# A seven-product group in the first two down-projection blocks, and shares that join the stream by adding transfers

## The chip, the cores and the metric

The kernel runs on one core of one Trainium2 chip. The metric is the device time of one execution in microseconds. Five engines work beside each other, each through its own program in order, and wait for each other by semaphores: PE (TensorE, matmuls), DVE (VectorE), ACT (ScalarE), POOL (GpSimd) and SP (SyncE, which here only issues transfers). Matmuls read SBUF and write PSUM, whose eight banks the kernel uses as `acc[0]`, `acc[1]` (two banks each) and `side` (four).

## The reference

The reference is a two-layer decoder trunk over 256 tokens with 2048 features: layer 0 is differential attention, layer 1 is attention over a shared latent K/V, and each layer ends in a squared-ReLU MLP with 8192 hidden features. The change is in the MLP only:

```
def sq_relu_mlp(h, w_up, w_down):
    return jnp.square(jax.nn.relu(h @ w_up)) @ w_down

x = x + sq_relu_mlp(rms_norm(x, mlp_norm_g[l]), w_up[l], w_down[l])
```

All is float32. The gains of the norm are in `opA` already, and the norm's per-token factor `rs` is applied where a product is added to the stream `xs`.

## The kernel before

**Halves.** The kernel gets float32 accuracy from three fast matmuls: each operand is split into a high part and a low part, and a product is high x high + high x low + low x high. A weight block is 2048 rows by 512 columns. SP loads it in four quads (`raw[:, r]`, 4 chunks of 128 rows, 1 MB each); each quad is two halves of two chunks. For each half ACT writes the high part (`whi`, L1080) and DVE subtracts it to make the low part (`wlo`, L1672); both are called `split(b, hf)`. `whi` and `wlo` are a ring of four halves, so ACT may write half n once PE has done half n - 4 (`pe_halves`). PE then does 12 matmuls of 128x512 for a half: 2 chunks, 2 token tiles, 3 products (`half_tok`, L595 to L597).

**Groups of seven products.** Where two weight blocks j and j+1 and the two token tiles form a 2x2 by 2x2 product, `seven` computes it with seven products instead of eight (Strassen's scheme in Winograd's form): 7 x 2 chunks x 3 = 42 matmuls (L828 to L830) instead of 48. Its names are B22, T1, B21, B11, T2, T3, T4, in PE's order. DVE makes the four weight sums in `w_sum` and in place in `raw` (L2199, L2202, L2209, L2213). Four of the seven weight operands go through the ring (ACT L1405, DVE L2188), three (T1, B11, T3) through `extra_hi` and `extra_lo` (ACT L1401, DVE L2182), which hold two; T3's high part takes T1's place and waits until PE has used it (`pe_extra`). The activations are combined too: `form_sums`, `form_high` and `form_low` make four sums and split them (`forms[0]`, `forms[1]`). Four of the products (T1, B11, T2, T3) land in the four `side` banks; they are shares of more than one output tile. ACT copies them out (`down_shared` in `junk` and `o_sb`, or `up_shared`), and `combine` on DVE turns them into the four tile sums by four 128x512 operations (L2105). The products that belong to one tile alone accumulate in `acc`.

**The MLP.** It runs in four quarters of the hidden features. In each quarter PE does four up blocks and four down blocks. Up blocks 2 and 3 of the first quarter and all up blocks of the others are done as `up_pair(q, i)`, with one seven-product group each. The results pass ReLU and square on ACT, are turned by DVE and by transfers (`up_turn`, `move_quads`, `hid_high`, `hid_low`) into `opB`. The down blocks are two stages. `first_down(q)` does down blocks 0 and 1, 16 plain halves in the order `DOWN_ORDER`. `pair(q)` does down blocks 2 and 3, with two seven-product groups in three of the quarters: four halves of block 2, group 0, two halves, group 1, two halves. After a block `add_scaled` (L2136) multiplies `acc` by `rs` and adds it to `xs`. The shares of `pair` are combined at its end, and `down_add` (L2251, two DVE operations over 128x1024) adds them to the stream in the next up pair. The last quarter has no group in its down blocks.

**Order.** All orders are written out by hand, per engine. PE runs the first three quarters in a `Fori` loop; ACT, DVE and SP are unrolled.

Of the kernel before, what the change touches and what calls it, by code (L numbers as in the profile page):

```python
# [39 lines left out]
NB = 512  # L40
# [45 lines left out]
IN_EXTRA = ("T1", "B11", "T3")  # L86
IN_RING = ("B22", "B21", "T2", "T4")
DOWN_ORDER = ((0, 0), (0, 1), (0, 2), (1, 0), (0, 3), (1, 1), (1, 2), (1, 3))
SUMS = {"T1": 1, "T3": 2, "T2": 3, "T4": 4}
PAIRS_UP = 2 * QUARTERS - 1  # L90
GROUPS = PAIRS_UP + 2 * (QUARTERS - 1)
SHARES = PAIRS_UP + QUARTERS - 1
# [3 lines left out]
def up_pairs(l, q, i):  # L96

    return PAIRS_UP * l + 2 * q - 1 + i


def up_groups(l, q, i):

    return GROUPS * l + 4 * q - 1 + i


def down_groups(l, q, g):
    return GROUPS * l + 4 * q + 1 + g


def up_shares(l, q, i):  # L110

    return SHARES * l + 3 * q - 1 + i


def down_shares(l, q):
    return SHARES * l + 3 * q + 1


def extra_place(l, at, form):

    return 2 * ((GROUPS * l + at + IN_EXTRA.index(form)) % 2)

# [37 lines left out]
def trunk(nc, x, positions, a_w_qkv, a_lambda, a_w_o, w_dkv, w_ukv, b_w_dq, b_w_uq, b_w_o, w_up, w_down,  # L160
# [11 lines left out]
    with ExitStack() as ctx:  # L172
# [196 lines left out]
        shared_sums = sem("shared_sums")  # L369
        shared_added = sem("shared_added")  # L370
# [17 lines left out]
        def _(sp):  # L388
# [53 lines left out]
            def mlp(l):  # L442
# [6 lines left out]
                def move_quads(q, j):  # L449

                    n = JB * (QUARTERS * l + q) + j
                    sp.wait_ge(sqT_done, n + 1)
                    if not (isinstance(n, int) and n == 0):
                        sp.wait_ge(hid_lo, 2 * n)
                    for a in range(4):
                        sp.dma_start(quads_moved[:, :, a, :], quads[32 * a:32 * a + 32, :]).then_inc(sq_moves, 16)

                def first_down(q):

                    b = B_MLP[l] + 2 * JB * q + JB  # L460
                    for k, (j, r) in enumerate(DOWN_ORDER):
# [5 lines left out]
                def pair(q):  # L467
# [3 lines left out]
                    for i, (j, r) in enumerate(order):  # L471
                        src = W_DOWN[l][:, KC * q + 4 * r:KC * q + 4 * r + 4, NB * j:NB * j + NB]
                        quad(b + i // 4, i % 4, src, later=int(i == 6))
# [61 lines left out]
        def _(pool):  # L535
# [21 lines left out]

            stream_scale(0)
            with pool.Fori(0, DA_PAIRS) as p:
                sub_norm(p)  # L560
            stream_scale(2)
            for k in range(2):
                pool.wait_ge(lat_ms, k + 1)
                nc.gpsimd.tensor_tensor(lrs[:, k, :], lms[:, k, :], neg_half[:, 0:TT], ALU.pow).then_inc(lat_rs, 1)
            for t in range(TT):
# [5 lines left out]
        def _(pe):  # L571
# [228 lines left out]
            def mlp(l, v_in):  # L800
# [3 lines left out]
                def seven(group, at, b, hf0, buf, c0, made, uses, opens, closes):  # L804
# [8 lines left out]
                    for f in FORMS:  # L813
                        shares = f in ("T1", "B11", "T2", "T3")
                        if f in IN_EXTRA:
                            pe.wait_ge(extra_lo_ready, len(IN_EXTRA) * group + IN_EXTRA.index(f) + 1)
                            hi, lo, place = extra_hi, extra_lo, extra_place(l, at, f)
# [4 lines left out]
                        first, last = opens and (shares or f == "B22"), closes and f != "B22"  # L822
                        if opens and f == "B22":
                            wait_bank(0, uses, 0)
# [8 lines left out]
                def shares_free(share):  # L833

                    if not (isinstance(share, int) and share == 0):
                        pe.wait_ge(shared_copied, 4 * share)

                def pair(q, uses):
# [4 lines left out]
                    shares_free(down_shares(l, q))  # L843
                    pe.wait_ge(form_lo, FORM_SETS * l + 2 * q + 3)
                    seven(down_groups(l, q, 0), 1, b, 4, opB, 8, [forms[0][:, i] for i in range(2)], uses[0], True, False)
                    for hf in range(2):
                        half_tok(b + 1, hf, 0, chunks_of(opB, 2 * hf), first=hf == 0, uses=uses[0], starts=(False, True))
                    seven(down_groups(l, q, 1), 2, b + 1, 2, opB, 12, [forms[1][:, i] for i in range(2)], None, False, True)
# [3 lines left out]
                def up_pair(q, i):  # L852
# [5 lines left out]
                    shares_free(up_shares(l, q, i))  # L858
                    pe.wait_ge(form_lo, FORM_SETS * l + 1)
                    seven(up_groups(l, q, i), i - 1, b, 6, opA, 0, x_forms, uses[0], True, True)  # L860
# [7 lines left out]
                def first_down(q):  # L868

                    b = B_MLP[l] + 2 * JB * q + JB  # L870
                    for k, (j, r) in enumerate(DOWN_ORDER):
# [1676 lines left out]
```

## Time and profile before

| | us |
|---|---|
| median of 3 runs | 1988.44 (1988.22 to 1989.09) |
| the profiled execution, its own time | 1988.36 |
| its span, from the first to the last instruction | 1986.6 |
| PE busy, 9128 matmuls | 1977.4 |
| DVE busy | 1582.4 |
| ACT busy | 1161.1 |
| POOL busy | 13.2 |

The busy times are sums over one execution; the engines work at the same time. PE's matmuls overlap each other, so the distance between their starts, not the duration of one, says how fast PE goes. A DVE or ACT operation likewise starts slightly before the one ahead of it has fully ended.

### The profile page before, as it was taken

How to read it: one execution, taken by the hardware profiler on the slowest of the kernel's cores; microseconds unless marked ns; L12 is line 12 of the kernel's file. 1: busy time of each engine (PE TensorE's matmuls, PEld its weight loads, DVE VectorE, ACT ScalarE, POOL GpSimd, SP SyncE). 2: the span in 40 equal slices, each digit the busy share in tenths (PEclk: the TensorE clock that was granted, in tenths of full speed). 3: DMA queues.
4: the chain of work that ended last, by engine and by line, in shares of the span. 5: the costliest groups of instructions: out<-in, count | busy, mean ns of one | idle time of the engine just before them, and what ended most of it. 6: DMA issues, size and time to landing. Idle time of an engine off the chain costs nothing.

```text
span 1986.6 us, 24882 instructions
## 1 busy us (share of the span) xinstructions
PE 1977.4 (100%) x9128; PEld 1651.8 (83%) x9128; DVE 1582.4 (80%) x1931; ACT 1161.1 (58%) x1481; POOL 13.2 (1%) x21
## 2 busy tenths in 40 slices
PE   9999999999999999999999999999999999999998
PEld 8888888888888888888888998888888888888887
DVE  7789996678888798788866787667798788889865
ACT  6555555556566456556656665556456556655653
POOL 0000000000000000000000000000000000000000
PEclk9999999999999999999999999999999999999999
DMA  8655546666566557656766554676557656656663
GB/s 307 212 170 189 182 157 216 225 194 234 190 215 223 191 200 241 220 190 202 242 212 195 143 152 151 223 229 223 181 194 240 223 199 212 227 186 212 212 240 106
DMA packets 265924, 405.26 MB, mean 204 GB/s; under 512 B 18416, under 2 KB 88432, under 8 KB 265840
## 3 DMA queue, kind: packets, MB, share of 16 engines
q1 hardware_dynamic: 251920, 395.82, 60.0%
q10 hardware_dynamic: 13920, 8.39, 1.5%
q8 instruction: 44, 0.72, 0.1%
q14 instruction: 40, 0.33, 0.0%
HBM read 379.00 MB, written 2.10 MB: 192 GB/s over the span
## 4 chain that ended last, share of the span: by engine, by line
PE 97%; issue 2%; DVE 1%; ACT 0%; POOL 0%; POOLq 0%; DVEq 0%; ACTq 0%
PE acc L595 24%; PE acc L597 24%; PE acc L596 24%; PE side L829 2%; PE side L830 2%; PE side L828 2%; PE acc L828 2%; PE acc L830 2%; PE acc L615 2%; PE acc L616 2%; PE acc L617 2%; PE acc L829 2%; PE acc L933 1%; PE acc L934 1%; PE acc L935 1%
## 5 line engine op out<-in xcount | busy, mean ns | idle before, releaser
L1672 DVE TENSOR_TENSOR wlo<-raw,whi 128x1024 fp32r<-128x1024 f32 (+1 forms) x596 | 709.7, 1206 | 214.7 <-ACT whi L1080 212.8
L1080 ACT ACTIVATE whi<-raw 128x1024 fp32r<-128x1024 f32 (+1 forms) x596 | 614.0, 1046 | 431.6 <-PE acc L597 360.4
L595 PE MATMUL acc<-whi,opB 128*128 128x512 f32 x1104 | 431.2, 391 | 0.1
L597 PE MATMUL acc<-whi,opB 128*128 128x512 f32 x1104 | 430.1, 390 | 0.0
L596 PE MATMUL acc<-wlo,opB 128*128 128x512 f32 x1104 | 429.9, 389 | 0.0
L595 PE MATMUL acc<-whi,opA 128*128 128x512 f32 (+2 forms) x1072 | 415.0, 387 | 0.0
L597 PE MATMUL acc<-whi,opA 128*128 128x512 f32 (+2 forms) x1072 | 414.2, 386 | 0.0
L596 PE MATMUL acc<-wlo,opA 128*128 128x512 f32 (+2 forms) x1072 | 414.1, 386 | 0.0
L597 PEld LDWEIGHTS acc<-whi,opB 128*128 128x128 f32 x1104 | 207.3, 188 | 43.2
L595 PEld LDWEIGHTS acc<-whi,opB 128*128 128x128 f32 x1104 | 207.4, 188 | 42.7 <-DVE wlo L1672 0.3
L596 PEld LDWEIGHTS acc<-wlo,opB 128*128 128x128 f32 x1104 | 207.4, 188 | 42.5
L597 PEld LDWEIGHTS acc<-whi,opA 128*128 128x128 f32 x1072 | 201.4, 188 | 40.0
L596 PEld LDWEIGHTS acc<-wlo,opA 128*128 128x128 f32 x1072 | 201.5, 188 | 39.8
L595 PEld LDWEIGHTS acc<-whi,opA 128*128 128x128 f32 x1072 | 201.5, 188 | 39.8
L1405 ACT ACTIVATE whi<-raw 128x1024 fp32r<-128x1024 f32 x78 | 82.9, 1063 | 96.5 <-DVE raw L2209 49.0
L1401 ACT ACTIVATE extra_hi<-raw 128x1024 fp32r<-128x1024 f32 x52 | 54.7, 1052 | 84.0 <-PE side L830 84.0
L2188 DVE TENSOR_TENSOR wlo<-raw,whi 128x1024 fp32r<-128x1024 f32 x78 | 95.1, 1219 | 0.0
L2182 DVE TENSOR_TENSOR extra_lo<-raw,extra_hi 128x1024 fp32r<-128x1024 f32 x52 | 63.6, 1222 | 23.1 <-ACT extra_hi L1401 23.1
L2087 DVE STREAM_TRANSPOSE o_sb<-junk 128x1024 f32<-128x1024 f32 x32 | 39.8, 1243 | 44.8 <-ACT junk L1359 44.8
L615 PE MATMUL acc<-whi,opA 128*128 128x512 f32 x184 | 72.0, 391 | 0.3 <-DVE wlo L1672 0.2
L616 PE MATMUL acc<-wlo,opA 128*128 128x512 f32 x184 | 71.7, 390 | 0.0
L617 PE MATMUL acc<-whi,opA 128*128 128x512 f32 x184 | 71.7, 389 | 0.0
(379 smaller groups left out, 2383.3 us busy)
## 6 DMA issues: line engine op xcount, KB each, us to landing
raw<-in_w_up SPq DMA_DIRECT2D x128, 1024.0 KB, 5.5
raw<-in_w_down SPq DMA_DIRECT2D x128, 1024.0 KB, 5.1
raw<-in_a_w_qkv SPq DMA_DIRECT2D x44, 1024.0 KB, 5.1
raw<-in_a_w_o SPq DMA_DIRECT2D x16, 1024.0 KB, 5.1
prob<-o_sb SPq DMA_DIRECT2D x128, 128.0 KB, 2.6
raw<-in_b_w_o SPq DMA_DIRECT2D x16, 1024.0 KB, 5.0
raw<-in_w_ukv SPq DMA_DIRECT2D x32, 256.0 KB, 4.2
prob<-o_sb ACTq DMA_DIRECT2D x48, 128.0 KB, 4.3
```

The source lines that it names most:

```text
L595: mm(o, a_hi, w_hi, start=start, stop=False)
L596: mm(o, a_hi, w_lo, start=False, stop=False)
L597: done = mm(o, a_lo, w_hi, start=False, stop=last and c == chunks - 1)
L615: mm(o, a_hi, whi[:, place, :], start=start, stop=False)
L616: mm(o, a_hi, wlo[:, place, :], start=False, stop=False)
L617: done = mm(o, a_lo, whi[:, place, :], start=False, stop=end)
L828: mm(o, a_hi, hi[:, place + c, :], start=first and c == 0, stop=False)
L829: mm(o, a_hi, lo[:, place + c, :], start=False, stop=False)
L1080: done = fn(whi[:, place:place + ch, 0:n], raw[:, r, c0:c0 + ch, 0:n], ACT.Copy)
L1405: fn(whi[:, 2 * (hf % 4):2 * (hf % 4) + 2, :], source[f], ACT.Copy).then_inc(hi_ready, 1)
L1672: done = tt_(wlo[:, place:place + ch, 0:n], raw[:, r, c0:c0 + ch, 0:n], whi[:, place:place + ch, 0:n].bitcast(F32), ALU.subtract)
L2188: tt_(wlo[:, places, :], src, whi[:, places, :].bitcast(F32), ALU.subtract).then_inc(lo_ready, 1)
```

## The change

`first_down` of three quarters gets a seven-product group in place of four plain quads: quads (0,0), (0,1), (1,0), (1,1) as plain halves, then the group on quads (0,2) and (1,2), then quads (0,3) and (1,3) plain. It uses `forms[0]`, which the first group of `pair` uses too, since both stand on hidden chunks 8 to 11; the form sums of both sets now come straight from `sqT`, and `rebuild` of `opB` goes. SP holds the next `move_quads` back until the first form sums are made.

The shares of the new group are copied by ACT at the end of `first_down` and combined by DVE in `pair`, between its first group and the next plain half. ACT then scales them by `rs` in place (`scale_shared`), and GpSimd issues two transfers that add them to the stream (`accum_op`). The shares of `pair` go the same way: they are combined where `down_add` stood, in the next up pair, scaled by ACT after the first operand of its group, and added by transfers. ACT waits for these transfers before it copies the next shares. PE's loop over the quarters is unrolled.

```diff
-DOWN_ORDER = ((0, 0), (0, 1), (0, 2), (1, 0), (0, 3), (1, 1), (1, 2), (1, 3))
+DOWN_FIRST = ((0, 0), (0, 1), (1, 0), (1, 1))
+DOWN_LAST = ((0, 3), (1, 3))
...
+            def shared_sums_added(l, key, c0):
+
+                nth = DOWN_SHARE[key]
+                q = key[2]
+                for s in range(2):
+                    pool.wait_ge(drained[s], 2 * (U_MLP[l][s] + U_QUARTER * q + U_UP + c0 // 2 + 1))
+                pool.wait_ge(shared_scaled, 2 * nth + 2)
+                for t, both in enumerate((junk[:].rearrange("p a n -> p (a n)"), o_sb[:].rearrange("p a t n -> p (a t n)"))):
+                    pool.dma_start(xs[:, t, NB * c0:NB * c0 + 2 * NB], both, accum_op=ALU.add).then_inc(shared_added, 16)
...
(PE, first_down)
+                    for k, (j, r) in enumerate(DOWN_FIRST):
+                        plain_quad(k, j, r)
+                    pe.wait_ge(hid_lo, n + 6)
+                    shares_free(SHARE["first", l, q])
+                    pe.wait_ge(form_lo, FORM_SETS * l + 2 * q + 2)
+                    seven(GROUP["first", l, q], b + 1, 0, opB, 8, [forms[0][:, i] for i in range(2)], None, True, SHARED)
+                    for k, (j, r) in enumerate(DOWN_LAST):
+                        plain_quad(6 + k, j, r)
 
-                with pe.Fori(0, QUARTERS - 1) as q:
+                for q in range(QUARTERS - 1):
...
(ACT)
+                def scale_shared(key):
+
+                    act.wait_ge(shared_sums, 4 * SHARE[key] + 4)
+                    act.wait_ge(rs_ready, 2 * l + 2)
+                    for t, both in enumerate((junk[:].rearrange("p a n -> p (a n)"), o_sb[:].rearrange("p a t n -> p (a t n)"))):
+                        fn(both, both, ACT.Copy, scale=rs[:, 2 * l + 1, t:t + 1]).then_inc(shared_scaled, 1)
...
                 def pair(q):
 
                     b = B_MLP[l] + 2 * JB * q + JB + 2
                     split(b, 3)
+                    seven(GROUP["down", l, q, 0], b, 4, (2, b), (3, b), {})
                     split(b + 1, 0)
                     split(b + 1, 1)
+                    scale_shared(("first", l, q))
+                    seven(GROUP["down", l, q, 1], b + 1, 2, (1, b + 1), (2, b + 1), {})
...
+                    act.wait_ge(shared_added, 32 * DOWN_SHARE["first", l, q] + 32)
+                    copy_shared()
...
(DVE)
+                def first_down(q):
+
+                    b, key = B_MLP[l] + 2 * JB * q + JB, ("first", l, q)
+                    uses = [u[s] + U_QUARTER * q + U_UP for s in range(2)]
+                    split(b, 3)
+                    up_turn(q, JB - 1)
+                    split(b, 4)
+                    hid_low(q, JB - 2)
+                    form_sums(sqT, down_set(q, 0))
+                    split(b, 5)
+
+                    def after_first():
+                        split(b, 6)
+                        form_low(down_form(0), down_set(q, 0))
+
+                    seven(GROUP[key], b + 1, 0, (0, b + 1), (1, b + 1), 8 * b + 3,
+                          {"first sum": after_first, "second sum": lambda: split(b, 7), "B11": lambda: hid_low(q, JB - 1)})
+                    split(b + 1, 4)
+                    form_sums(sqT, down_set(q, 1))
...
                 def pair(q):
...
+                    seven(GROUP["down", l, q, 0], b, 4, (2, b), (3, b), 8 * b + 3, {"first sum": lambda: split(b, 3)})
+                    combine(SHARE["first", l, q], down_shared)
                     split(b + 1, 0)
...
-                    combine(down_shares(l, q), down_shared)
                     add_scaled(b + 1, 0, 2 * uses[0], slice(3 * NB, 4 * NB))
...
                         if follows == "down":
-                            down_add(q - 1)
+                            combine(SHARE["down", l, q - 1, 0], down_shared)
```

## Rows read from the trace of the kernel before

**Rows 1.** The page, part 1: busy time, share of the span and count.
```profile
PE 1977.4 (100%) x9128; PEld 1651.8 (83%) x9128; DVE 1582.4 (80%) x1931; ACT 1161.1 (58%) x1481; POOL 13.2 (1%) x21
```
**Rows 2.** Waits of PE: line, waited for, us in total, times, longest.
```profile
PE side L648 <- DVE junk L1827: 1.1, 1, 1.1
PE acc L664 <- ACT whi L1159: 0.2, 1, 0.2
PE acc L615 <- DVE wlo L1672: 0.2, 1, 0.2
```
**Rows 3.** Windows: us, then PE, PEld, DVE, ACT, POOL busy, PEclk, DMA share, GB/s.
```profile
465.00:509.00 44.00, 44.00 (x196) 36.46 (x195) 32.28 (x35) 23.83 (x23) 0.00 (x0) 1.00 0.66 219
509.00:536.00 27.00, 27.00 (x120) 22.18 (x119) 24.59 (x23) 15.25 (x15) 0.00 (x0) 1.00 0.55 179
```
**Rows 4.** Timeline of PE: start, duration, operation; first matmuls of stages and groups.
```profile
465.61 0.39 PE L595 MATMUL acc<-whi,opB 128*128 128x512 f32 x1
...
509.13 0.39 PE L595 MATMUL acc<-whi,opB 128*128 128x512 f32 x1
...
520.02 0.40 PE L828 MATMUL acc<-whi,v_hl 128*128 128x512 f32 x1
...
529.75 0.39 PE L595 MATMUL acc<-whi,opB 128*128 128x512 f32 x1
...
539.39 0.39 PE L828 MATMUL side<-extra_hi,opB 128*128 128x512 f32 x1
...
550.39 0.39 PE L595 MATMUL acc<-whi,opA 128*128 128x512 f32 x1
```
**Rows 5.** Timeline of DVE in `pair`: T3, half 0; B11, T3; stream addition.
```profile
524.17 1.23 DVE L2182 TENSOR_TENSOR extra_lo<-raw,extra_hi 128x1024 fp32r<-128x1024 f32 x1 [2.07 <-ACT extra_hi L1401]
...
526.44 1.22 DVE L1672 TENSOR_TENSOR wlo<-raw,whi 128x1024 fp32r<-128x1024 f32 x1
...
536.66 1.22 DVE L2182 TENSOR_TENSOR extra_lo<-raw,extra_hi 128x1024 fp32r<-128x1024 f32 x1
...
539.35 1.22 DVE L2182 TENSOR_TENSOR extra_lo<-raw,extra_hi 128x1024 fp32r<-128x1024 f32 x1 [0.33 <-ACT extra_hi L1401]
...
545.14 1.41 DVE L2136 SCALAR_TENSOR_TENSOR xs<-acc,rs,xs 128x512 f32<-128x512 f32 x2 [1.16 <-PE acc L830]
```
**Rows 6.** Timeline of ACT in `pair`: T3 and T4, then B22 of the second group.
```profile
523.08 1.06 ACT L1401 ACTIVATE extra_hi<-raw 128x1024 fp32r<-128x1024 f32 x1 [4.42 <-PE side L830]
524.04 1.05 ACT L1405 ACTIVATE whi<-attn_both 128x1024 fp32r<-128x1024 f32 x1
...
527.23 1.06 ACT L1405 ACTIVATE whi<-raw 128x1024 fp32r<-128x1024 f32 x1 [0.25 <-PE side L830]
```
**Rows 7.** Timeline of DVE: `combine` first row, stream addition, `down_add`, the half after.
```profile
550.33 0.68 DVE L2105 TENSOR_TENSOR o_sb<-o_sb,junk 128x512 f32<-128x512 f32 x1
...
553.11 1.40 DVE L2136 SCALAR_TENSOR_TENSOR xs<-acc,rs,xs 128x512 f32<-128x512 f32 x2
...
556.70 1.28 DVE L2251 SCALAR_TENSOR_TENSOR xs<-junk,rs,xs 128x1024 f32<-128x1024 f32 x1
...
559.09 1.22 DVE L1672 TENSOR_TENSOR wlo<-raw,whi 128x1024 fp32r<-128x1024 f32 x1
```
**Rows 8.** Timeline around the one wait of PE for a low part.
```profile
50.77 1.23 DVE L1672 TENSOR_TENSOR wlo<-raw,whi 128x1024 fp32r<-128x1024 f32 x1 [2.37 <-ACT whi L1080]
...
51.54 0.39 PE L617 MATMUL acc<-whi,opA 128*128 128x512 f32 x1
...
52.38 0.40 PE L616 MATMUL acc<-wlo,opA 128*128 128x512 f32 x1
```
**Rows 9.** The page, part 5: ACT from `o_sb` into `junk`.
```profile
L1364 ACT ACTIVATE junk<-o_sb 128x1024 f32<-128x1024 f32 x14 | 28.7, 2052 | 24.7 <-DVE o_sb L2111 24.7
```
**Rows 10.** The page, part 6: transfers by line, count, KB each, us to landing.
```profile
raw<-in_w_down SPq DMA_DIRECT2D x128, 1024.0 KB, 5.1
...
prob<-o_sb SPq DMA_DIRECT2D x128, 128.0 KB, 2.6
```

More of the change, by code:

```diff
@@ L821, in seven @@
                             hi, lo, place = whi, wlo, 2 * (hf % 4)
-                        first, last = opens and (shares or f == "B22"), closes and f != "B22"
-                        if opens and f == "B22":
+                        first, last = opens and (shares or f == "B22" and uses is not None), f in closes
+                        if opens and f == "B22" and uses is not None:
                             wait_bank(0, uses, 0)
@@ L833, in shares_free @@
                 def shares_free(share):
-                    if not (isinstance(share, int) and share == 0):
+                    if share:
                         pe.wait_ge(shared_copied, 4 * share)
@@ L1379, in form_high, with down_forms, copy_shared, seven @@
                     fn(made, form_raw, ACT.Copy).then_inc(form_hi, 1)
-                def down_forms(q, g, nth):
-                    form_high(forms[g][:, 0], FORM_SETS * l + 2 * q + nth + 1)
-                def seven(group, at, b, hf0, own, other, between):
+                def down_forms(q, g):
+                    form_high(forms[g][:, 0], FORM_SETS * l + 2 * q + g + 1)
+                def copy_shared():
+                    for k in range(4):
+                        fn(down_shared[k], side[k], ACT.Copy).then_inc(shared_copied, 1)
+                def scale_shared(key):
[3 more added lines that the diff above has]
+                        fn(both, both, ACT.Copy, scale=rs[:, 2 * l + 1, t:t + 1]).then_inc(shared_scaled, 1)
+                def seven(group, b, hf0, own, other, between):
                     (o, o_loads), (t, t_loads) = own, other
@@ L1420, in pair @@
                     split(b + 2, 1)
-                    for k in range(4):
-                        fn(down_shared[k], side[k], ACT.Copy).then_inc(shared_copied, 1)
+                    act.wait_ge(shared_added, 32 * DOWN_SHARE["first", l, q] + 32)
+                    copy_shared()
                     split(b + 2, 2)
@@ L1434, in up_pair @@
                     split(b, 5)
-                    between = {} if after == "down" else {"T4": lambda: hid_high(q, 2 * i - 1)}
-                    seven(up_groups(l, q, i), i - 1, b, 6, (3, b), (0, b + 1), between)
+                    between = {"T4": lambda: hid_high(q, 2 * i - 1)}
+                    if after == "down":
+                        between = {"B22": lambda: scale_shared(("down", l, q - 1, 0))}
+                    seven(GROUP["up", l, q, i], b, 6, (3, b), (0, b + 1), between)
                     for hf in range(2, 6):
@@ L2188, in low, with seven @@
                         tt_(wlo[:, places, :], src, whi[:, places, :].bitcast(F32), ALU.subtract).then_inc(lo_ready, 1)
[L2190 removed]
+                def seven(group, b, hf0, own, other, lows_before, after):
                     (o, o_loads), (t, t_loads) = own, other
[L2193 removed]
+                    n, e = 4 * group, 3 * group
                     b11, b21 = raw[:, o, 0:2, :], raw[:, o, 2:4, :]
@@ L2209, in seven @@
                     tt_(b22, w_sum, b22, ALU.add).then_inc(w_summed, 1)
-                    low("B21", group, at, b, hf0, b21)
+                    low("B21", group, b, hf0, b21)
                     dve.wait_ge(w_summed, n + 3)
```

197 lines of the change are left out of this document (110 added, 87 removed).

## The prediction

> **What bounds the kernel now.** I read the busy rows of the page first: PE 1977.4 us of a span of 1986.6 [rows 1], at a granted clock of 1.00 in the stages around the change [rows 3]. Then PE's own waits: three in the whole execution, 1.5 us together, none in an MLP [rows 2]. So the sum is PE's stream of matmuls, and a change counts in two ways only: by the matmuls it drops, and by each moment at which it makes PE wait for a weight half. VectorE (DVE) supplies those halves (`wlo`, `extra_lo`); its busy time is 80% of the span [rows 1], but that is a mean. By stage, in the second half of the down-projection (the function `pair`), it is 24.59 us of 27 [rows 3]. So I read PE's and DVE's rows of `pair` side by side [rows 4, 5] to see how early each half is ready.
>
> **What it removes: matmuls.** The first two down-projection blocks run 16 halves of 12 matmuls from 465.61 to 509.13 us, 2.72 us a half, 10.88 us for the four halves of two weight quads. A seven-product group has 42 matmuls instead of 48 and runs from 520.02 to 529.75, 9.73 us [rows 4]; all 26 groups of the trace take 9.73 or 9.74. One new group saves 10.88 - 9.73 = 1.15 us. There are 3 quarters in 2 layers, 6 new groups: 6.9 us. By this alone, the profiled execution's 1988.36 us (span 1986.6 plus 1.76 around it, and 0.08 from the median 1988.44) becomes 1981.5.
>
> **What it adds in `first_down`.** DVE gets four weight sums, three more low parts and no `rebuild` of the activations; ScalarE (ACT) three more high parts; each 128x1024 op holds DVE for 1.14 us and ACT for 0.96, start to start [rows 5, 6]. I laid these rows into the new order, counting from PE's first matmul of the stage (0 = 465.61). DVE starts at 1.4 with half 3, waits for ACT's squares until 4.5 as before, and runs on: half 4, `hid_low`, form sums (1.5), half 5, first sum at 10.6, half 6, form low part, second sum, half 7 done at 16.3 (PE needs it at 19.0), B22 17.4 (21.8), T1 18.6 (23.2), B21 20.9 (24.5), B11 23.1 (25.9), T2 25.5 (27.3), T3 27.1 (28.7), T4 28.2 (30.1), the four plain halves from 29.3 (31.5) on. The smallest lead is T3's, 1.6 us, the lead that T3 has in the present groups too: its high part waits until PE has used T1's buffer [rows 6], so it can't be earlier. No wait; the stage ends with DVE waiting for PE at the stream addition, as now. I price it at 0. The bounds: no gain is possible here beyond the 1.15, since PE has no wait to lose, so the low end is 0; one DVE operation more than laid out still fits the lead of 1.6, two would be late by 0.7 per group.
>
> **What it adds in `pair`: the step that decides.** The four operations that turn the new group's shares into sums (`combine`) stand on DVE between the first group of `pair` and half 0 of the next block. Today's four run from 550.33 and the next operation starts at 553.11: 2.78 us [rows 7]. Nothing there hides them. T3's low part starts at 524.17 only because its high part waits for PE [rows 5, 6]; the 2.07 us that DVE idles ahead of it come before the `combine` and stay unused. From 524.17 DVE has no gap until 539.02: T4 525.31, half 0 526.44, sum, half 1, sum, B22, T1, sum, B21, sum, B11 536.66 to 537.88, T2, then 0.33 idle at T3 [rows 5]. PE starts half 0 at 529.75 and B11 at 539.39 [rows 4]. With 2.78 more, half 0 is ready at 527.66 + 2.78 = 530.44, 0.69 after PE wants it, and B11 at 537.88 + 2.78 = 540.66, 1.27 after.
> What a late half costs beyond its lateness shows where PE once waited: low part ready at 52.00, matmul due at 51.77 (51.54 plus one interval of 0.227), and the matmul after it at 52.38 instead of 51.99, so 0.39 lost for 0.23 late, 0.16 more [rows 8]. PE's stream is thus pushed by 0.69 + 0.16 = 0.85 at half 0 and to 1.27 + 0.16 = 1.43 in all at B11; T2 then has 0.3 left, T3 0.5. Behind them DVE waits for PE again (the 1.16 us idle before 545.14 [rows 5]), so nothing carries over. All six pairs show these rows at the same offsets within 0.02 us. Cost: 6 x 1.43 = 8.6 us. Bounds: 0, if the slack that I read isn't PE's real limit; 2.78 a pair if none of it can be used; I take 1.43, from rows of the same instructions.
> ACT gets `scale_shared`, two passes over 128x1024, ahead of the second group's B22. They start when `combine` ends, 529.3, and take 1.06 each by ACT's other rows of this size from SBUF [rows 6], to 531.4; B22's high part (now 527.23 [rows 6]) is ready at 532.4, and DVE comes to it at 533.8. Hidden. The dearest like row, 2.05 us for 128x1024 from `o_sb` into `junk` [rows 9], would make it 534.4 and add 0.6 a pair.
>
> **The shares' way into the stream.** `down_add`'s two DVE operations (556.70 to 559.09, 2.39 us) go, and a `combine` of 2.78 stands in their place, while the `combine` at the end of `pair` (2.78) goes [rows 7]. That end is no longer late against PE (DVE's addition at 553.11 could have started at 550.39), so the up pair's first sum comes about 1.5 us earlier relative to PE. No gain: PE did not wait there. Instead GpSimd, which is idle (13.2 us busy [rows 1]), issues two 512 KB adding transfers per share, 24 in all, 12.6 MB against 405. They queue on POOL behind nothing that is late (`stream_scale` of that layer is over; that of the next waits for the MLP's end anyway). Behind the new waits: ACT's wait for `shared_added` ahead of the share copies (547, shifted), with half 2 of the next block and all later high parts behind it; copies could be about 3 us later. First share: issue near 531.5, limit near 551, 19 us. Second: scaled after the up group's first high part, 562, limit near 580, 18 us. No row shows an adding transfer. The nearest: 1024 KB from HBM in 5.1 us, 128 KB from SBUF to SBUF in 2.6 [rows 10]. Two of 512 KB are then between 5.1 and 8 x 2.6 = 21 us if four pieces of 128 KB each went one after the other; four of the latter were issued together and overlap, so I take 5 to 10, hidden. The weight load with the least margin there, for the first sum of the second group (used just after half 0), is over before the adding transfers start.
>
> The page "DMA: Bandwidth & Descriptors" of the Trainium skill (Anatomy of one DMA) gives about 2.0 us plus bytes/436 GB/s for a GpSimd-issued transfer: an estimate of 3.2 us each, without saying what the adding costs. "SBUF — State Buffer" (Who interferes with whom) has a rule that speaks against this change: descriptors of such transfers are written by GpSimd through the port pair it shares with VectorE, and VectorE in a two-port mode shuts it out; it also says that `tensor_tensor` has no such mode. By the first, the transfers are hidden; if the lock held all the while that DVE works without a gap (524 to 539), they would start 8 us later, still inside 19. No run here shows it so far.
>
> **Unrolled PE loop.** The `Fori` over quarters on PE becomes straight code. PE's starts show no step over 0.3 us at the loop's edges now, and the last quarter is straight code already without a wait; price 0.
>
> **Sum.** 1988.44 - 6.9 + 8.6 = 1990.1 us.
>
> **Rivals.**
> (A) The forecast: PE waits about 1.4 us in every pair, what the group gave goes back. For it: the gapless DVE rows. 0.60, range 1987 to 1993.
> (B) DVE's lateness does not reach PE, the whole 6.9 us are kept: 1981.5. For it: no PE wait in any MLP today. Against: the leads are 1.5 to 2.1 us and the insertion 2.78. With half the stall, 1985.8. 0.17.
> (C) The other side: the adding transfers are slow, and ACT's wait stops the high parts. It decides from about 19 us for two of them; at 25 us each of 12 waits loses 6 us: 1990.1 + 72 = 2062; at 20 us, 1990.1 + 12 = 2002. For it: no row of such a transfer, DMA share 0.55 to 0.67 in these stages [rows 3]. Against: 5.1 us a megabyte. 0.10.
> (D) `first_down` or ACT's scaling is tighter than laid out, 0.6 to 1.1 us per quarter on top of A: 1990.1 + 3.6 to 6.8, 1993.7 to 1996.9. 0.13.
>
> **How the numbers follow.** Likeliest is A, 1990.1. What this kernel can tell from no change is about 0.2%, 4.0 us: 1984.5 to 1992.4. A lies in it but for 0.05 above; B gives 0.15 faster, 0.02 inside; C is slower; D 0.10 slower and 0.03 inside. With that, faster 0.15, same 0.60, slower 0.25. The range takes in B's 1981.5 at its low end, since B and C together outside it would be more than 2 in 10, and reaches to D's lower half: 1981.2 to 1995, with C and the rest of D left out.
>
> **What would show it.** Right: six PE waits of about 0.6 us on a `wlo` low part at half 0 after the first group of `pair`, and six at `extra_lo` for B11 in the second group, each after an unbroken row of DVE operations with the four of `combine` in it; 36 fewer PE matmuls; `first_down` 42.4 us instead of 43.52, without a wait; the stage from 509.13 to 550.39 longer by 1.4. Wrong: PE without such waits (B); ACT idle ahead of L1422's copies, released by a DMA (C); waits at T2 to T4 in `first_down` or at B22 in the second group of `pair` (D).

## The result, and the profile after

| | us | |
|---|---|---|
| before | 1988.92 | median of 14 runs, 1988.22 to 1989.73 |
| changed | 1993.33 | median of 14 runs, 1991.10 to 1995.36 |
| ratio | 1.0023 | 95% interval 1.0015 to 1.0031 |
| changed, profiled execution | 1994.45 | span 1992.6 |

The changed kernel is 4.4 us slower, by 0.23%. The interval of the ratio leaves out 1, and the size is about the 0.2% that the prediction took as the least that can be told from no change. The forecast was 1990.1 (1981.2 to 1995). Profiled execution against profiled execution the span grew by 6.0 us, 1986.6 to 1992.6.

The page's busy line and its software queue, after (before: [rows 1]):

```profile
PE 1976.1 (99%) x9092; PEld 1643.0 (82%) x9092; DVE 1620.8 (81%) x1979; ACT 1209.8 (61%) x1547; POOL 34.3 (2%) x45
...
q0 software_dynamic: 3456, 12.58, 3.6%
```

36 matmuls are gone (9128 to 9092), DVE has 38 us more to do, and 12.58 MB go through GpSimd's queue. Next the waits of PE in the changed kernel (line, waited for, us in total, times, longest), which answer to [rows 2]:

```profile
PE acc L608 <- DVE wlo L1733: 4.7, 8, 0.6
PE side L842 <- DVE extra_lo L2239: 1.6, 6, 0.3
PE side L661 <- DVE junk L1888: 1.1, 1, 1.1
PE acc L628 <- DVE wlo L1733: 0.8, 2, 0.6
```

The `junk` wait was there before. Twelve of the others are the predicted ones, two in each of six `pair` stages. The remaining two `wlo` waits of the first line were not predicted. The last line is in the first 31 us, before any changed stage (section 3 of the experiments). This view leaves out gaps of PE under 0.15 us; where such a gap matters below, it is read from the distances between PE's starts. PE's timeline of the same stages as in [rows 4], after; the second number is the duration, the bracket the wait:

```profile
466.79 0.39 PE L608 MATMUL acc<-whi,opB 128*128 128x512 f32 x1
...
488.56 0.40 PE L842 MATMUL acc<-whi,v_hl 128*128 128x512 f32 x1
...
498.29 0.39 PE L608 MATMUL acc<-whi,opB 128*128 128x512 f32 x1
...
509.18 0.39 PE L608 MATMUL acc<-whi,opB 128*128 128x512 f32 x1
...
529.57 0.40 PE L844 MATMUL acc<-whi,opB 128*128 128x512 f32 x1
530.54 0.50 PE L608 MATMUL acc<-whi,opB 128*128 128x512 f32 x1 [0.58 <-DVE wlo L1733]
530.88 0.39 PE L609 MATMUL acc<-wlo,opB 128*128 128x512 f32 x1
...
540.08 0.40 PE L844 MATMUL acc<-whi,opB 128*128 128x512 f32 x1
540.76 0.50 PE L842 MATMUL side<-extra_hi,opB 128*128 128x512 f32 x1 [0.29 <-DVE extra_lo L2239]
541.10 0.39 PE L843 MATMUL side<-extra_lo,opB 128*128 128x512 f32 x1
...
563.46 0.50 PE L608 MATMUL acc<-whi,opA 128*128 128x512 f32 x1 [0.58 <-DVE wlo L1733]
```

`first_down` is 42.39 us (466.79 to 509.18) instead of 43.52, its group 9.73, and it has no wait. In `pair` half 0 starts 0.97 after the matmul before it instead of 0.23, and the next interval is 0.34: 0.74 + 0.11 = 0.85 lost. B11 loses 0.45 + 0.11 = 0.56 more. Together 1.41 per `pair`, the same within 0.03 in all six. DVE's timeline in that stage, against [rows 5]:

```profile
524.21 1.23 DVE L2239 TENSOR_TENSOR extra_lo<-raw,extra_hi 128x1024 fp32r<-128x1024 f32 x1 [2.07 <-ACT extra_hi L1440]
525.35 1.22 DVE L2245 TENSOR_TENSOR wlo<-attn_both,whi 128x1024 fp32r<-128x1024 f32 x1
526.49 0.69 DVE L2166 TENSOR_TENSOR o_sb<-o_sb,junk 128x512 f32<-128x512 f32 x1
...
528.66 0.69 DVE L2166 TENSOR_TENSOR o_sb<-junk,o_sb 128x512 f32<-128x512 f32 x1
529.27 1.22 DVE L1733 TENSOR_TENSOR wlo<-raw,whi 128x1024 fp32r<-128x1024 f32 x1
...
539.49 1.22 DVE L2239 TENSOR_TENSOR extra_lo<-raw,extra_hi 128x1024 fp32r<-128x1024 f32 x1
```

The four `combine` operations (L2166) move half 0 from 526.44 to 529.27 and B11 from 536.66 to 539.49, 2.83 each, and no gap stands between them. The 2.07 us of idle time ahead of T3 are still there, in front of the `combine` and of no use to it.

The third kind of wait, at 563.46, is that of half 4 in the up pair that follows (`up_pair`, whose DVE order is first sum, `combine`, half 4). DVE's timeline there:

```profile
553.37 1.21 DVE L1733 TENSOR_TENSOR wlo<-raw,whi 128x1024 fp32r<-128x1024 f32 x1
...
558.26 1.23 DVE L2256 TENSOR_TENSOR attn_both<-raw 128x1024 f32<-128x1024 f32 x1 [3.69 <-issue]
559.41 0.68 DVE L2166 TENSOR_TENSOR o_sb<-o_sb,junk 128x512 f32<-128x512 f32 x1
...
562.19 1.22 DVE L1733 TENSOR_TENSOR wlo<-raw,whi 128x1024 fp32r<-128x1024 f32 x1
```

DVE is idle for 3.69 us and then late. "issue" names no releaser; the first sum (L2256) needs a weight quad, so I looked at the weight loads. The load issued at 550.30, in the view of transfers of that moment (KB each, us to landing):

```profile
raw<-in_w_up SPq DMA_DIRECT2D x1, 1024.0 KB, 7.9
```

It lands at 558.2, where the idle time ends. The load in its place before was issued at 548.85 and took 5.1 us, to 553.9. In the changed kernel it is the last of four that are issued 541.87, 544.14, 546.41 and 550.30 (before: 539.05, 541.74, 544.01, 548.85). With a low part ready at 563.4 half 4 comes late by 0.7. This wait costs 0.85, 0.91 and 0.24 us in three of the six up pairs (563.46, 1483.10, 1653.27), 2.0 in all; in a second execution of the same kernel one of them alone stood (below).

A late load is not the whole of it. DVE also idles ahead of this first sum where `pair` is on time, in the kernel with the early `combine` (section 1), and hardly does where the share of `pair` goes its old way (section 2). The same instruction in these two:

```profile
555.53 1.22 DVE L2256 TENSOR_TENSOR attn_both<-raw 128x1024 f32<-128x1024 f32 x1 [2.52 <-issue]
555.22 1.22 DVE L2254 TENSOR_TENSOR attn_both<-raw 128x1024 f32<-128x1024 f32 x1
```

Over all kernels in which this share goes by transfer the idle time is 2.1 to 3.7 us in every up pair of this kind. It opens because the `combine`, 2.8 us, has left the end of `pair`, where it stood while the load was landing, and now stands behind the load. The lateness of `pair` comes on top; with both, half 4 has no lead.

### The profile page after: what moved, and what is told of

Read it like the earlier page. It is cut to its first block, busy times and chain, and to the rows that moved or that the text cites. A ratio compares the mean times of both kernels' runs of the same rounds, so it can differ in the third digit from the quotient of the medians.

```text
span 1992.6 us, 24530 instructions
## 1 busy us (share of the span) xinstructions
PE 1976.1 (99%) x9092; PEld 1643.0 (82%) x9092; DVE 1620.8 (81%) x1979; ACT 1209.8 (61%) x1547; POOL 34.3 (2%) x45
## 3 DMA queue, kind: packets, MB, share of 16 engines
q0 software_dynamic: 3456, 12.58, 3.6%
## 4 chain that ended last, share of the span: by engine, by line
PE 89%; DVE 5%; issue 4%; DMA 1%; ACT 1%; POOL 0%; POOLq 0%; DVEq 0%; ACTq 0%
PE acc L608 22%; PE acc L609 22%; PE acc L610 22%; PE side L842 2%; PE side L844 2%; PE side L843 2%; PE acc L628 2%; PE acc L629 2%; PE acc L630 2%; PE acc L842 2%; PE acc L844 2%; PE acc L843 2%; DVE wlo L1733 1%; DVE wlo L2245 1%; DVE extra_lo L2239 1%
## 5 line engine op out<-in xcount | busy, mean ns | idle before, releaser
L1733 DVE TENSOR_TENSOR wlo<-raw,whi 128x1024 fp32r<-128x1024 f32 x572 | 679.9, 1205 | 167.6 <-ACT whi L1108 165.8
L1108 ACT ACTIVATE whi<-raw 128x1024 fp32r<-128x1024 f32 x572 | 586.8, 1045 | 350.9 <-PE acc L610 280.8
L608 PE MATMUL acc<-whi,opB 128*128 128x512 f32 x1008 | 394.2, 391 | 3.5 <-DVE wlo L1733 3.5
L610 PE MATMUL acc<-whi,opB 128*128 128x512 f32 x1008 | 392.5, 389 | 0.0
L609 PE MATMUL acc<-wlo,opB 128*128 128x512 f32 x1008 | 392.3, 389 | 0.0
L608 PEld LDWEIGHTS acc<-whi,opB 128*128 128x128 f32 x1008 | 189.2, 188 | 45.2 <-DVE wlo L1733 6.3
L610 PEld LDWEIGHTS acc<-whi,opB 128*128 128x128 f32 x1008 | 189.2, 188 | 39.7
L609 PEld LDWEIGHTS acc<-wlo,opB 128*128 128x128 f32 x1008 | 189.2, 188 | 38.6
L1444 ACT ACTIVATE whi<-raw 128x1024 fp32r<-128x1024 f32 x96 | 101.7, 1059 | 98.0 <-PE acc L610 54.9
L1440 ACT ACTIVATE extra_hi<-raw 128x1024 fp32r<-128x1024 f32 x64 | 67.3, 1052 | 92.5 <-PE side L844 92.5
L2245 DVE TENSOR_TENSOR wlo<-raw,whi 128x1024 fp32r<-128x1024 f32 x96 | 117.0, 1218 | 0.0
L2239 DVE TENSOR_TENSOR extra_lo<-raw,extra_hi 128x1024 fp32r<-128x1024 f32 x64 | 78.1, 1221 | 21.9 <-ACT extra_hi L1440 21.8
```

Of the source, the lines that this page charges most:

```text
L608: mm(o, a_hi, w_hi, start=start, stop=False)
L609: mm(o, a_hi, w_lo, start=False, stop=False)
L610: done = mm(o, a_lo, w_hi, start=False, stop=last and c == chunks - 1)
L1108: done = fn(whi[:, place:place + ch, 0:n], raw[:, r, c0:c0 + ch, 0:n], ACT.Copy)
L1444: fn(whi[:, 2 * (hf % 4):2 * (hf % 4) + 2, :], source[f], ACT.Copy).then_inc(hi_ready, 1)
L1733: done = tt_(wlo[:, place:place + ch, 0:n], raw[:, r, c0:c0 + ch, 0:n], whi[:, place:place + ch, 0:n].bitcast(F32), ALU.subtract)
```

## The experiments

All ratios are to the kernel before, run on the same chip. Each diff is cut to its core; where nothing else is said it is one against the changed kernel.

**1. The late `combine`, moved, shrunk, and the transfers shrunk.** Three edits by themselves, two of them together, and the loop unrolled in the kernel before.

`combine` ahead of T3's low part, that is in the 2.07 us of idle time:

```
                     low("T2", group, b, hf0, b22)
+                    if "T2" in after:
+                        after["T2"]()
                     low("T3", group, b, hf0, b12)
...
-                    seven(GROUP["down", l, q, 0], b, 4, (2, b), (3, b), 8 * b + 3, {"first sum": lambda: split(b, 3)})
-                    combine(SHARE["first", l, q], down_shared)
+                    seven(GROUP["down", l, q, 0], b, 4, (2, b), (3, b), 8 * b + 3,
+                          {"first sum": lambda: split(b, 3), "T2": lambda: combine(SHARE["first", l, q], down_shared)})
```

> Edit: in the first group of `pair`, the new group's four combine operations stand on VectorE ahead of T3's low part, where it idled 2.07 us, not behind T4's. Theory S (the late operation list): 2.07 of the 2.78 us are covered, T3's low part is 0.7 us later than in the kernel before, still 0.9 ahead of TensorE; half 0 and B11 of the second group are ready before TensorE wants them. The six pairs of waits (0.85 and 0.56 us each in the changed kernel, 8.5 us) go: 1993.3 - 8.5 = 1984.8; the weight loads move back about 2 us too, and with them the late halves 4 of the up pairs (2.0 us in the profile): about 1983, below the kernel before by 5 to 6 us. Rival R (the adding transfers slow the weight loads): the waits in `pair` go, those at half 4 of the up pairs stay, about 1985, and the single runs spread over 3 to 4 us as they do in the changed kernel.

Measured: 1985.79 us (11 runs, 1983.51 to 1990.07), ratio 0.9987 [0.9978, 0.9996]. Not one of the twelve waits in `pair` is left: they were the `combine`'s place. Half 4 is never late. But three new waits stand at 761 to 776 us, 1.5 us lost, behind ScalarE's copies of the shares, which waited for an adding transfer. The time is near the 1985 of rival R, but not by its mechanism, which had the waits at half 4 stay. GpSimd's timeline of that kernel:

```profile
730.90 0.85 POOL L562 DMA_DIRECT2D xs<-junk  x1 [31.22 <-ACT o_sb L1421]
740.13 0.88 POOL L562 DMA_DIRECT2D xs<-o_sb  x1 [8.37 <-issue]
```

And ScalarE's:

```profile
748.40 0.60 ACT L1505 ACTIVATE junk<-side 128x512 f32<-128x512 f32 x1 [2.33 <-DMA xs<-o_sb]
```

The second of the two transfers was issued 9.2 us behind the first and landed 17.4 us after the first's issue.

`combine` on 8 of 512 columns:

```
-                    combine(SHARE["first", l, q], down_shared)
+                    combine(SHARE["first", l, q], [part[:, 0:8] for part in down_shared])
```

> Edit: the new group's combine works on 8 of 512 columns (left out: the sums of that group's shares outside them). It keeps its place, its count and its semaphores. Theory S: the four operations take about 0.6 us instead of 2.78, B11's low part is ready 0.9 us before TensorE wants it: no waits in `pair`, and the loads are less bunched: 1993.3 - 8.5 - 2 = 1983. If something else than VectorE's time made TensorE wait there (scaling on ScalarE, a transfer), the waits stay and the time is above 1988.

Measured: 1984.41 us (11 runs, 1983.01 to 1988.93), ratio 0.9979 [0.9970, 0.9988]. No wait in any `pair`, at the same place in the order: it is its 2.8 us of work and not its waits. One up pair lost 2.2 us, again behind an adding transfer that landed late (17.5 us), and half 4 of another lost 0.2. The expectation was 1983.

Adding transfers of 16 of 1024 columns:

```
-                    pool.dma_start(xs[:, t, NB * c0:NB * c0 + 2 * NB], both, accum_op=ALU.add).then_inc(shared_added, 16)
+                    pool.dma_start(xs[:, t, NB * c0:NB * c0 + 16], both[:, 0:16], accum_op=ALU.add).then_inc(shared_added, 16)
```

> Edit: each adding transfer moves 16 of its 1024 columns (left out: most of the addition of the shares to the stream). Theory S: the waits in `pair` stay at 1.41 us each; at half 4 of the up pairs the four weight loads issued within 9 us (541.87 to 550.30) are still bunched, the last still takes about 8 us, and the waits there stay: 1993 within 1. Rival R: the first sum of the up pair's group comes without its 2.3 to 3.7 us of idle time, no wait at half 4, and about 2 us less: 1991; the spread of single runs shrinks to the 1.5 us of the kernel before.

Measured: 1993.38 us (9 runs, 1992.79 to 1996.15), ratio 1.0025 [1.0015, 1.0035], as the changed kernel; the waits in `pair` are 1.41 each as before, and half 4 is late in three up pairs, 1.0 us in all. In the changed kernel as it stands the transfers' size costs nothing that can be measured.

Both edits, `combine` ahead of T3 and small transfers:

> Edits: the new group's combine ahead of T3's low part (as e1) and adding transfers of 16 of 1024 columns (as e2; left out: most of the addition of the shares). Theory S+R (VectorE's order costs the waits in `pair`, the full-size adding transfers cost the late loads in the up pairs and the spread): 1988.9 - 6.9 + 0.8 for the unrolled loop = 1982.8, single runs within 1.5 us of each other instead of the 6.6 of e1. If the spread comes from the changed load order and not from the transfers: 1985 to 1986 with e1's spread.

Measured: 1983.31 us (8 runs, 1982.29 to 1984.38), ratio 0.9973 [0.9963, 0.9984], no wait in an MLP. Against the early `combine` alone it is 2.5 us less: once DVE is on time, the transfers are what is late.

The unrolled loop on PE in the kernel before:

```
-                with pe.Fori(0, QUARTERS - 1) as q:
+                for q in range(QUARTERS - 1):
```

> Edit: the kernel before with TensorE's loop over the quarters unrolled, nothing else. Theory S: nothing, 1988.9 within 0.5. Rival U (the longer program costs something, for example in fetching instructions beside the first loads, where the changed kernel's profile is 1.1 us later at 290 us, before any changed stage): 1989.5 to 1990.5.

Measured: 1989.65 us (11 runs, 1988.88 to 1991.53), ratio 1.0003 [0.9994, 1.0012]. By the interval no difference can be told. But the median is 0.8 us above the 1988.86 of the 31 runs beside it, all 11 runs lie above that median, and the time is what rival U expected, not theory S. In the profile PE is 0.9 us later than in the kernel before at the first `first_down`, nearly all of it lost by 36 us.

**2. The other share as it was.** The changed kernel, with the share of the old group combined at the end of `pair` and added by DVE in `down_add`, as in the kernel before; only the new group's share goes by transfer (12 instead of 24). Once with the new `combine` late, as in the change, and once ahead of T3:

```
-                    shared_sums_added(l, ("down", l, q, 0), 2)
...
+                    combine(SHARE["down", l, q, 0], down_shared)
                     add_scaled(b + 1, 0, 2 * uses[0], slice(3 * NB, 4 * NB))
...
-                            combine(SHARE["down", l, q - 1, 0], down_shared)
+                            down_add(q - 1)
```

Late:

> Edit: only the second half of e7, the combine of the new group stays behind T4's low part as in the changed kernel. Theory: the waits in `pair` stay at 1.41 us each, the others go: 1988.9 - 6.9 + 8.5 + 0.8 = 1991.3, with a spread under 2 us, and without waits at half 4 of the up pairs. Rival (the late halves 4 come from the bunched loads after a late `pair`, whoever adds): 1993.

Measured: 1991.43 us (11 runs, 1990.25 to 1993.40), ratio 1.0014 [1.0005, 1.0023]. The waits in `pair` are there, 1.41 each; none at half 4. The last load of `pair` takes 7.3 us here, the first sum waits 0.60 and starts at 556.59 instead of 558.26, and with two operations of 2.4 us in all behind it instead of four of 2.8 half 4's low part starts at 560.12 instead of 562.19. The rival, bunched loads whoever adds, is out: the loads are as bunched as in the changed kernel. So 1.9 us of the change's time lie in the new way of this share, by the medians; the intervals of the two ratios overlap, so the size is rough.

Ahead of T3:

> Edits: combine ahead of T3's low part (as e1), and the shares of `pair` go the way of the kernel before: combine at the end of `pair`, two additions on VectorE in the up pair, no adding transfers there; the new group's share keeps its transfers, 12 in all. Theory: VectorE had room for this in the kernel before, the transfers that ran into ACT's share copies of the up pair are gone: 1982.8, spread under 2 us; below the kernel before by 6 us. Rival: the remaining transfers beside the next weight loads delay them as much: 1985 to 1986 as e1.

Measured: 1982.67 us (6 runs, 1982.05 to 1983.11), ratio 0.9969 [0.9957, 0.9982]; nothing is left out of the computation. It is faster than both kernels, by 0.3% and 0.5%. Its DVE timeline:

```profile
521.51 0.69 DVE L2166 TENSOR_TENSOR o_sb<-o_sb,junk 128x512 f32<-128x512 f32 x1
...
523.68 0.69 DVE L2166 TENSOR_TENSOR o_sb<-junk,o_sb 128x512 f32<-128x512 f32 x1
524.29 1.22 DVE L2237 TENSOR_TENSOR extra_lo<-raw,extra_hi 128x1024 fp32r<-128x1024 f32 x1
...
536.78 1.22 DVE L2237 TENSOR_TENSOR extra_lo<-raw,extra_hi 128x1024 fp32r<-128x1024 f32 x1
```

The `combine` fills the idle time, T3 starts at 524.29 as in [rows 5], 524.17, and B11 at 536.78 against 536.66. The late one differs from this kernel by the place of the `combine` alone: 1991.43 - 1982.67 = 8.8 us, the term that the prediction had at 8.6.

**3. Which waits stay from run to run.** The kernel before and the changed kernel once more, unedited.

> The kernel before, unchanged, for a second profile: theory U (the unrolled loop costs 0.8 us at the start) expects no wait of TensorE near 30 us, where all five profiles with an unrolled loop have one of 0.6 to 0.8 us; if it shows here too, that wait is chance and the loop costs nothing.

Measured: 1988.95 us (10 runs). No wait stands near 30 us, as theory U expects; but the wait does not belong to the unrolled loop for certain either, for three of the other kernels with it, the small transfers with the early `combine`, the late version of 2 and the one of section 4, have none there.

> The changed kernel, unchanged, beside e9 on one chip, for a second profile: six pairs of waits of 1.41 us in `pair`, as in the first; the waits at half 4 of the up pairs vary, 0 to 0.9 each; the wait near 30 us is there or not, as in the kernels e5 and e8 it was not.

Measured: 1993.28 us (7 runs), ratio 1.0028 [1.0017, 1.0040]. All twelve waits in `pair` are there again; of the waits at half 4 only one, 0.89 us at 1482.01. So the waits in `pair` are fixed and those at half 4 stand on an edge. One more thing moves between kernels: what PE loses in the first 36 us, most of it in one wait near 30 us, in a stage that no edit touches. Against the first profile of the kernel before, PE reaches the first `first_down` 1.2 us later in both profiles of the changed kernel, 0.9 in the kernel before with its loop unrolled, 0.2 in the repeat of before, 0.6 and 0.1 in the early and the late version of 2. With the loop it is 0 to 0.2, unrolled 0.1 to 1.2. The longer program is a suspect; what sets it stays open.

**4. Half 4 ahead of the `combine`.** It should take away the waits at half 4 and nothing else.

```
                     def after_first():
+                        if follows != "down":
+                            up_turn(q, 2 * i - 1)
+                        split(b, 4)
                         if follows == "down":
                             combine(SHARE["down", l, q - 1, 0], down_shared)
-                        else:
-                            up_turn(q, 2 * i - 1)
-                        split(b, 4)
```

> Edit: in the up pair after `pair`, VectorE makes half 4's low part ahead of the combine of the down share instead of behind it; nothing else. Theory L (the first weight sum there waits 2.3 to 3.7 us for the last of four bunched loads, and the combine of 2.78 then stands ahead of half 4): the waits at half 4 (0.2 to 0.9 us, 2.0 in the changed kernel's profile) go, half 5 may be 0.1 to 0.4 late where the load is latest: 1992 beside 1993.3 of the changed kernel. If the 1.9 us between the changed kernel and the one whose down share is added by VectorE come from the adding transfers holding up ACT's copies, nothing changes: 1993.3.

Measured: 2000.21 us (5 runs, 1999.48 to 2001.56), ratio 1.0059 [1.0045, 1.0073]. My expectation of 1992 failed by 8 us. The waits at half 4 are gone; ten others, 7.8 us lost, came later in three up pairs, after ScalarE's copies had waited for the adding transfers, 10.0 us in three waits. GpSimd's timeline of one such share in the changed kernel:

```profile
565.07 0.85 POOL L562 DMA_DIRECT2D xs<-junk  x1 [30.91 <-ACT o_sb L1421]
571.36 0.89 POOL L562 DMA_DIRECT2D xs<-o_sb  x1 [5.44 <-issue]
```

The same share here:

```profile
564.92 0.85 POOL L562 DMA_DIRECT2D xs<-junk  x1 [31.61 <-ACT o_sb L1421]
573.84 0.89 POOL L562 DMA_DIRECT2D xs<-o_sb  x1 [8.07 <-issue]
```

ScalarE's timeline here, at the copies:

```profile
582.51 0.60 ACT L1505 ACTIVATE junk<-side 128x512 f32<-128x512 f32 x1 [4.05 <-DMA xs<-o_sb]
```

The first transfer is issued at the same moment and takes 8.7 us instead of 6.0; the second, which starts behind it, 8.6 instead of 4.9. What differs is the weight load beside them. SyncE's timeline of the changed kernel:

```profile
565.71 0.37 SPq L385 DMA_DIRECT2D raw<-in_w_up  x1
```

And of this one:

```profile
564.42 0.37 SPq L385 DMA_DIRECT2D raw<-in_w_up  x1
```

With half 4 earlier its buffer is free earlier, and the load goes 0.5 us ahead of the adding transfer instead of 0.6 behind it; the next load follows 7.9 us later and meets the second. The issue times and landings of the second share of each quarter, the one that is scaled in the up pair, give one table for both kernels:

| second transfer | load behind the first transfer | load ahead of it |
|---|---|---|
| held until the first landed | both down after 11.2 to 11.3 us (3 shares, changed kernel) | 16.2 to 17.5 us (3 shares, this one) |
| not held | 10.9 to 12.3 us (3) | 11.0 to 12.3 us (3) |

Both must meet: held and beaten by the load. This is read off the shares; neither condition was changed alone. The two late shares of section 1 (17.4 and 17.5 us) were held ones too, with the load 0.3 us behind the first issue and at the same moment. ScalarE's copies come 15 us after the first issue (580.03 in the changed kernel), so 11 is hidden and 17 is not.

The same kernel with transfers of 16 columns tells whether their bytes are the whole cause:

> The changed kernel with half 4 split ahead of the combine in the up pair (as in the run that took 2000.2 us), and with adding transfers that move 16 of the 1024 columns of each row only (so the stream lacks most of the shares; the transfers' count, waits and order stay). In the 2000.2 us run the waits that were new lay in the up pairs in which the second adding transfer was held until the first had landed, and there a weight load was issued 0.5 us ahead of the first adding transfer instead of 0.6 us behind it; the first took 8.4 to 8.9 us instead of 6.0 to 6.2, both were down after 16 to 17.5 us instead of 11.2, and ScalarE's copies waited up to 4.1 us for them. Theory L (the bytes of the adding transfers, sharing the engines with that weight load, are the whole cause): both are down after some 6 to 8 us, ScalarE never waits for them, no PE wait at half 4 and none later in the up pairs; what is left are the waits of the group's combine, 1.4 us in each of six pairs: 1988.8 - 6.9 + 8.5 + about 1 = 1991.4 (1990 to 1993). Rival (the order of DVE's work after half 4 is itself too late, the transfers only add to it): waits at several low parts of the up pairs stay and the time is 1994 or more.

Measured: 1992.17 us (10 runs, 1991.12 to 1993.77), ratio 1.0017 [1.0008, 1.0027]. Both transfers are down after 7.4 us at most, ScalarE waits for none, and the view of waits has only the twelve of `pair` in the MLPs:

```profile
PE acc L608 <- DVE wlo L1733: 3.5, 6, 0.6
PE side L842 <- DVE extra_lo L2239: 1.6, 6, 0.3
```

The rival, an order of DVE that is itself too late, is out as the cause of the 8 us. A small part of it is true: PE's starts show half 5 late in three up pairs (565.19, 1654.03, 1824.33), by gaps under 0.15 us, 0.95 us lost in all, so this order moves the lateness from half 4 to half 5. 8.0 us of this experiment's 2000.2 came with the bytes of 12.6 MB of transfers, which the changed kernel hides with 3.8 us to spare in the share shown.

## Why the prediction was right, and where it was not

**The forecast's main case, rival A, holds in its mechanism.** The group saves 1.15 us (10.88 - 9.73), 36 matmuls are gone, and the late `combine` gives it back: 1.41 measured per `pair` against 1.43, with 0.85 at half 0 against 0.85. The clean measure of it is the pair of kernels of experiment 2, 8.8 us against 8.6. The 0.16 us beyond lateness that one wait of [rows 8] gave was right too. What made it come out was to lay DVE's rows and PE's starts side by side, and to see that an idle gap ahead of an inserted step isn't slack for it. The time itself is 0.3 us above the range that the prediction gave to rival A, 1987 to 1993. It lies in the full range because that was widened for the lower half of rival D, which did not come. That is luck; the terms that took its place are below.

**`first_down`** costs nothing, as laid out: T3's low part, the tightest, starts 25.9 us after the stage's first matmul and is ready at 27.1, as in the layout:

```profile
492.71 1.23 DVE L2239 TENSOR_TENSOR extra_lo<-raw,extra_hi 128x1024 fp32r<-128x1024 f32 x1 [0.52 <-ACT extra_hi L1440]
```

**ScalarE's scaling** took 1.06 us each, start to start, and B22's high part behind it is ready at 532.5, laid out for 532.4:

```profile
529.39 1.15 ACT L1421 ACTIVATE junk<-junk,rs 128x1024 f32<-128x1024 f32 x1 [2.36 <-DVE o_sb L2166]
530.45 1.14 ACT L1421 ACTIVATE o_sb<-o_sb,rs 128x1024 f32<-128x1024 f32 x1
531.49 1.04 ACT L1444 ACTIVATE whi<-raw 128x1024 fp32r<-128x1024 f32 x1
```

So rival D is out, and so is rival B, by the twelve waits.

**The step that failed** is "The shares' way into the stream", where the up pair was priced with "No gain: PE did not wait there", that is at 0. The prediction had the first sum come about 1.5 us earlier against PE. It came 1.2 later: 6.4 us after the stage's first matmul (558.26 and 551.84) instead of 5.2 (555.56 and 550.39). I asked only whether the end of `pair` came earlier, and not when the first sum's weight quad would land. The old `combine` had covered that landing; with it gone from there DVE idles 3.69 us for the load, and then the `combine` of 2.78, in place of `down_add`'s 2.39, stands ahead of half 4. DVE's lateness in `pair` moves the load too: the four are issued at shorter distances, and the last takes 7.9 us instead of 5.1. In the kernel before with its loop unrolled the same load takes 5.9 to 6.6 at the old distances, so the shorter distances need not be the whole of that. Missed size: 1.9 us by the medians (1993.3 against 1991.4). In the profiles the waits at half 4 are 2.0 and 0.9, and 0.6 more lie at the very end: from the start of the last matmul to the end of the span it is 8.5 us in every kernel with 24 adding transfers, whatever their size, and 7.8 to 7.9 in all others. Why was not tried.

**The adding transfers** were priced as hidden, and in the change they are. The numbers behind that were off. I took 5 to 10 us for the two and a limit of 18 or 19; they take 10.8 to 12.4, and the limit is 15. In five of twelve shares the second is held until the first has landed, but those not held take as long. The page "DMA: Bandwidth & Descriptors" of the Trainium skill (Anatomy of one DMA) gave an estimate of 3.2 us for one; no transfer of this size here took less than 4.5, median 6.2 and 10.4 for the first and second. "SBUF — State Buffer" of the Trainium skill (Who interferes with whom) says that `tensor_tensor` has no two-port mode, the kind that shuts GpSimd out. The trace agrees: at 532.21, in the middle of DVE's stretch without a gap, which is all `tensor_tensor`, GpSimd issued both within 0.73 us, and DVE's operations kept their 1.22 us. Rival C's mechanism is real all the same: in the early `combine` it costs 2.5 us and in experiment 4 it costs 8.0. There a load 1.1 us earlier was enough.

**The sum.** Against the forecast the median is 3.2 us higher. 0.5 of it is the base, 1988.92 here instead of 1988.44, and 1.9 is the missed step. The last 0.8 is the size by which the unrolled loop raised the kernel before, priced at 0. It fits the other kernels too, though no interval confirms it: experiment 2 gains 6.1 us by the medians without any wait in an MLP, not 6.9, and the expectations of both its kernels and of the two edits together in section 1, which had 0.8 for the loop, came out within about 0.5 us. In the profiled executions the span's growth of 6.0 is -6.8 (`first_down`, six times 1.13), 8.5 for `pair`, 2.0 at half 4, 1.2 in the first 36 us and 0.6 behind the last matmul; the other 0.5 are spread over steps too small to name.

## What to carry to other kernels

- A saving of matmuls in a stream that is fed by another engine is worth its time only if what it adds there is put where that engine idles. Here the same four operations cost 8.8 us behind T3 and nothing in front of it. Idle time can be used by what stands before the instruction that waits, and by nothing behind it.
- A step that is moved away may have covered someone's wait for a load. Look at what stood beside the landing, and put nothing that the next consumer must pass behind the wait that opens.
- When an engine that frees buffers gets later, look at the transfers that it releases: how close together they are then issued, and which other transfer gets ahead of which. Price the consumer of the last one anew, even where nothing waited before.
- A transfer that is "hidden" has a lead too. Measure it at its consumer and compare it with its slowest landing beside other traffic, not with its median alone.

## What the runs showed of the hardware that was not expected

- Two adding transfers of 512 KB from SBUF to SBUF, issued by GpSimd one behind the other, take 10.8 to 12.4 us together in the changed kernel. Single ones take 4.5 to 11.8 us; with 16 of 1024 columns 2.0 to 6.3 in the three kernels that have them.
- In shares 2, 4, 5, 8 and 11 of the 12 GpSimd issued the second only when the first had landed, with 512 KB 5.7 to 9.2 us later; in the others 0.5 to 0.7 us later. It was the same five in every profile with 24 transfers, whatever their size or place; with 12 transfers it was shares 2, 4 and 5. So it goes by the number in the queue and not by the traffic or the bytes. Why was not tried.
- With a 1024 KB load issued between 0.6 us ahead of the first 512 KB transfer of a share and 0.35 behind it, that transfer took 8.4 to 9.6 us; with 0.39 and 0.45 behind 8.0 and 7.2; with 0.48 behind or later 5.5 to 6.8, but for the first share of the execution with the load 0.6 behind, 7.9 to 8.2.
- Of four 1024 KB loads issued over 8.4 to 8.5 us the last took 6.4 to 7.9 us in the two profiles of the changed kernel; over 9.8 us 5.1 to 5.8 in the two of the kernel before, but 5.9 to 6.6 in the one with its loop unrolled.
- A late operand costs PE 0.16 us beyond its lateness, in all six half-0 waits as in the one of [rows 8]: 0.69 late, 0.85 lost. At B11 it is 0.40 late, 0.56 lost.
